# Two transformer blocks in fp32: the first projection unit of a layer before tile 1's transposes, and seven other operations moved

## The reference, cut to what matters

```python
for l in range(2):                                   # first block
    h = rmsnorm(x, pre_g[l]);  proj = h @ w_in[l]     # 2816 columns: u, v, g_a, q, k, v, g_b
    y_a = u * (spatial_w[l] applied to layernorm(v), + spatial_b) * silu(g_a)
    y_b = attention(rope(rmsnorm(q)), rope(rmsnorm(k)), v) * silu(g_b)     # 8 heads, 2 key heads
    x = x + rmsnorm(concat(y_a, y_b) @ w_out[l], post_g[l])
h = concat(zeros(112), meta_tokens(16), x)           # second block
proj = rms_norm(h, gain) @ w_in_2                    # 6400 columns
o_sb = stick_breaking_attention(8 heads)             # exp(log_beta + suffix sums of log(1 - beta))
o_sw = sliding_window_attention(16 heads, 2 key heads, sinks, rope)
merged = sigmoid(g_sb) * ((o_sb*silu(sb_z)) @ w_branch_sb) + sigmoid(g_sw) * ((o_sw*silu(sw_z)) @ w_branch_swa)
out = rms_norm(h + merged @ w_out_2, final_gain)     # rows of x alone
```

## Time and profile before

| what | value |
|---|---|
| profiled execution | 1017.53 us, span 1015.7 us, mean granted TensorE clock 0.997 |
| runs | 1016.79, 1018.24, 1018.8 us |
| TensorE (PE) busy | 982.3 us, 97% of the span |
| VectorE (DVE) busy | 618.0 us, 61% |
| ScalarE (ACT) busy | 497.8 us, 49% |
| GpSimd (POOL) busy | 265.0 us, 26% |
| DMA | 80.44 MB, 79 GB/s over the span |

### The profile page before, as it was taken

One profiled execution on the slowest core, in us unless ns is written; L12 is line 12 of the kernel. 1 busy time (PEld: TensorE's weight loads), 2 busy tenths in 40 slices (PEclk: granted clock), 3 DMA queues, 4 the chain that ended last, 5 costly groups with the idle time before them and its releaser, 6 DMA issues.

```text
span 1015.7 us, 13806 instructions
## 1 busy us (share of the span) xinstructions
PE 982.3 (97%) x5015; PEld 824.1 (81%) x5015; DVE 618.0 (61%) x917; ACT 497.8 (49%) x887; POOL 265.0 (26%) x198
## 2 busy tenths in 40 slices
PE   6999999999999999999999999999999989999996
PEld 5988888787888888787788889888787768888885
DVE  4777678928777678928336586588558962212204
ACT  4445656525445656525457577423557972222222
POOL 2216100003216100003322031140325764224242
PEclk9999999999999999999999999999999999999999
DMA  8332201231432101241322020023310003323312
GB/s 282 115 106 77 70 22 43 83 125 56 136 116 91 55 21 43 83 152 34 122 83 83 1 71 24 33 83 102 105 58 7 27 16 104 104 84 104 125 41 83
DMA packets 66790, 80.44 MB, mean 79 GB/s; under 512 B 5520, under 2 KB 50704, under 8 KB 66720
## 3 DMA queue, kind: packets, MB, share of 16 engines
q1 hardware_dynamic: 64816, 76.64, 23.4%
q10 hardware_dynamic: 1904, 2.88, 0.8%
HBM read 77.42 MB, written 2.10 MB: 78 GB/s over the span
## 4 chain that ended last, share of the span: by engine, by line
PE 56%; issue 29%; DVE 7%; ACT 4%; POOL 2%; DMA 1%; POOLq 0%; ACTq 0%; DVEq 0%
PE ps L1837 15%; PE ps L1839 15%; PE ps L1838 15%; DVE pwt L1516 2%; PE ps L1888 1%; PE ps L1890 1%; PE ps L1889 1%; PE ps L2175 1%; DVE wr L1613 1%; DVE yw L1732 1%; ACT whi L894 1%; PE ps L2323 1%; DMA x<-in_x 1%; POOL small L533 1%; POOL small L535 1%
## 5 line engine op out<-in xcount | busy, mean ns | idle before, releaser
L578 POOL TENSOR_TENSOR wlo<-raw,whi 128x2048 fp32r<-128x2048 f32 (+1 forms) x27 | 119.8, 4436 | 293.2 <-ACT whi L894 293.2
L1837 PE MATMUL ps<-whi,hhi 128*128 128x512 f32 (+1 forms) x320 | 116.4, 364 | 3.6 <-DVE wlo L1191 1.3
L1839 PE MATMUL ps<-whi,hlo 128*128 128x512 f32 (+1 forms) x320 | 114.9, 359 | 0.0
L1838 PE MATMUL ps<-wlo,hhi 128*128 128x512 f32 (+1 forms) x320 | 114.8, 359 | 0.0
L1837 PE MATMUL ps<-hhi,whi 128*128 128x512 f32 x288 | 113.3, 393 | 0.0
L1838 PE MATMUL ps<-hlo,whi 128*128 128x512 f32 x288 | 112.3, 390 | 0.0
L1839 PE MATMUL ps<-hhi,wlo 128*128 128x512 f32 x288 | 112.3, 390 | 0.0
L894 ACT ACTIVATE whi<-raw 128x2048 fp32r<-128x2048 f32 (+1 forms) x35 | 63.6, 1816 | 94.0 <-PE ps L1839 93.9
L660 ACT ACTIVATE whi<-raw 128x2048 fp32r<-128x2048 f32 (+1 forms) x29 | 52.2, 1800 | 72.8 <-PE ps L1839 72.8
L1191 DVE TENSOR_TENSOR wlo<-raw,whi 128x2048 fp32r<-128x2048 f32 (+1 forms) x29 | 63.6, 2192 | 35.9 <-ACT whi L660 35.1
L1888 PE MATMUL ps<-hhi,whi 128*128 128x512 f32 x192 | 78.2, 407 | 0.0
(11 more groups left out here) (310 smaller groups left out, 2332.4 us busy)
## 6 DMA issues: line engine op xcount, KB each, us to landing
raw<-in_w_in SPq DMA_DIRECT2D x42, 1024.0 KB, 5.3
raw<-in_w_out SPq DMA_DIRECT2D x12, 1024.0 KB, 5.0
raw<-in_w_in SPq DMA_DIRECT2D x10, 512.0 KB, 4.1
raw<-in_w_branch_swa SPq DMA_DIRECT2D x4, 1024.0 KB, 5.0
raw<-in_w_branch_sb SPq DMA_DIRECT2D x4, 512.0 KB, 3.4
x<-in_x ACTq DMA_DIRECT2D x3, 512.0 KB, 5.9
out<-x SPq DMA_DIRECT2D x3, 512.0 KB, 2.6
ws<-in_spatial_w SPq DMA_DIRECT2D x2, 512.0 KB, 6.7
```

Source lines behind the costliest of these rows:

```text
L578: pool.tensor_tensor(wlo[s][:, 0:n, :], raw[s][:, 0:n, :], whi[s][:, 0:n, :].bitcast(F32), ALU.subtract).then_inc(slab_split, 1)
L1837: pe.matmul(out_ap, lhsT=lhi(k), rhs=rhi(k), start=first and k == 0, stop=False, skip_group_check=True)
L1838: pe.matmul(out_ap, lhsT=lhi(k), rhs=rlo(k), start=False, stop=False, skip_group_check=True)
L1839: m = pe.matmul(out_ap, lhsT=llo(k), rhs=rhi(k), start=False, stop=last and k == n - 1, skip_group_check=True)
```

## The change

At the start of a layer unit (0,0) becomes a function, `first_unit`, that runs between the transposes of tile 0 and tile 1 at the program's start, and as the last thing in the loop's body for the layer (or block) that follows; the loops over `FIRST_UNITS` skip it. The identity transposes at the start become 12. ScalarE rounds the first piece of slab 0 ahead of tile 1's square sum, and VectorE takes its low part and tile 0's first half ahead of normalising tile 1. VectorE's low part of tile 3 moves from the loop's end to its top, and the low part of slab 2 ahead of the rope tables. `mix_low` and the gate's multiply move behind `read_head`. The meta tokens get a semaphore of their own. In the stick-breaking heads VectorE's `sb_read` moves ahead of `qk_parts`, and ScalarE's `copy_low_part` ahead of `meta_keys_hi` in head 1 and behind two copies at the end. The turned keys and queries are rounded ahead of a slab, and the low part of slab 34 moves from GpSimd to VectorE.

```diff
--- before
+++ after
@@ -358,6 +358,7 @@
         final_loaded = sem("final_loaded")
+        meta_loaded = sem("meta_loaded")
         start_done, consts_ready = sem("start_done"), sem("consts_ready")
@@ -494,7 +495,7 @@
             late(consts_f[:], a["consts"])
-            late(meta_row[:], a["meta_tokens_2"])
+            sp.dma_start(meta_row[:], a["meta_tokens_2"]).then_inc(meta_loaded, 16)
             for c in range(2):
@@ -622,9 +623,9 @@
             for j in range(21, len(SLABS2)):
-                if j in DVE_SLABS:
+                if j in DVE_SLABS or j == 34:
                     continue
-                if j - 1 in DVE_SLABS:
+                if j - 1 in DVE_SLABS or j == 35:
@@ -691,10 +692,10 @@
             sum_x(0, 0, 0)
+            first_slab_hi(0, 0, 0)
             act.wait_ge(x_loaded[1], 16)
...
             load_x(2)
-            first_slab_hi(0, 0, 0)
             load_x(3)
@@ -900,11 +901,12 @@
-            act.wait_ge(late_loaded, 128)
+            act.wait_ge(meta_loaded, 16)
             act.activation(junk[0:META, :], meta_row[:], ACT.Square, scale=ROOT, accum_out=small2[0:META, 0:1])\
...
             transposed_x(DEPTH, 0, 3)
+            act.wait_ge(late_loaded, 112)
             split2(2)
@@ -989,11 +991,11 @@
                         qk_parts(4 + h)
-                    if h == 1:
-                        meta_keys_hi(1)
                     if h in (4, 5):
...
                     copy_low_part(h)
+                    if h == 1:
+                        meta_keys_hi(1)
                 if h in (2, 3, 5):
@@ -1005,11 +1007,12 @@
             copy(sprm[:, 0, :], spm[:]).then_inc(sprm_hi, 1)
-            copy_low_part(7)
+            act.wait_ge(sbo_done, 8)
             for i in range(2):
...
                      ps[:, i, :].rearrange("p (t n) -> p t n", t=2)).then_inc(tokw_copied, 1)
+            copy_low_part(7)
             unit(29)
@@ -1046,10 +1049,10 @@
                 act.activation(tgz(c), ps[:, 6 + c % 2, :], ACT.Tanh, scale=0.5).then_inc(z_tanh, 1)
+                for p in TURNS_AT[c]:
+                    tokens_transposed_hi(p)
                 if c % 2 == 1 and c < 7:
                     split2(15 + c // 2)
-                for p in TURNS_AT[c]:
-                    tokens_transposed_hi(p)
             act.wait_ge(rope2_done, 5)
@@ -1195,9 +1198,9 @@
             normalise(0, 0, 0)
-            normalise(0, 0, 1)
             first_slab_low(0, 0, 0)
             transposed_x(0, 0, 0, (0,))
+            normalise(0, 0, 1)
             first_slab_low(0, 0, 1)
@@ -1205,8 +1208,9 @@
             transposed_x(0, 0, 2)
-            transposed_x(0, 0, 3)
             with dve.Fori(0, DEPTH) as l:
+                transposed_x(l, 0, 3)
+
                 count = [FIRST]
@@ -1218,6 +1222,7 @@
+                slab_low(l, 2)
                 dve.wait_ge(gain_loaded, l * 96 + 96)
@@ -1290,7 +1295,6 @@
-                slab_low(l, 2)
                 turned(0)
@@ -1395,6 +1399,13 @@
+                def open_gate(c):
+
+                    dve.wait_ge(gb_tanh, l * 4 + c + 1)
+                    dve.scalar_tensor_tensor(gb[:, c, :], eb[:, 1, :], 1.0, gb[:, c, :], ALU.add, ALU.mult)\
+                       .then_inc(gate_ready, 1)
+                    dve.wait_ge(gate_ready, l * 4 + c + 1)
+
                 def mix_slab_low_of(piece):
@@ -1430,12 +1441,17 @@
                     else:
+                        mix_low(2)
                         mix_slab_low_of(0)
...
                         read_head(h - 1)
+                    if h in (6, 7):
+                        mix_low(h - 6)
+                    if h % 2:
+                        open_gate(h // 2)
                     if h < 8:
@@ -1448,15 +1464,6 @@
                         probabilities_low(h, 3)
-                        if h >= 5:
-                            mix_low(h - 5)
-                        if h % 2 == 0:
-
-                            c = h // 2
-                            dve.wait_ge(gb_tanh, l * 4 + c + 1)
-                            dve.scalar_tensor_tensor(gb[:, c, :], eb[:, 1, :], 1.0, gb[:, c, :], ALU.add, ALU.mult)\
-                               .then_inc(gate_ready, 1)
-                            dve.wait_ge(gate_ready, l * 4 + c + 1)
@@ -1494,7 +1501,6 @@
                 transposed_x(l, 1, 2)
-                transposed_x(l, 1, 3)
                 a["chain"].append(count[0] - FIRST)
@@ -1516,9 +1522,10 @@
-            dve.wait_ge(late_loaded, 128)
             dve.wait_ge(meta_root, 1)
             dve.tensor_scalar(meta_row[:], meta_row[:], small2[0:META, 1:2], None, ALU.mult).then_inc(start_done, 1)
+            transposed_x(DEPTH, 0, 3)
+            dve.wait_ge(late_loaded, 112)
             dve.tensor_copy(rows_of[:], consts_f[:, CONSTS - 8:])
@@ -1615,6 +1622,7 @@
                     terms_lo(h + 1)
+                    sb_read(h)
                     if h < 4:
@@ -1627,8 +1635,8 @@
                     low(sprm[:, 1, :], spm[:], sprm[:, 0, :]).then_inc(sprm_lo, 1)
-                sb_read(h)
                 if h == 7:
+                    sb_read(h)
                     dve.wait_ge(meta_summed, 1)
@@ -1803,6 +1811,8 @@
+            slab2_low(34)
+
             def final_norm(t):
@@ -1851,9 +1861,23 @@
             pe.wait_ge(const_loaded, 16)
-            for n in range(16):
+            for n in range(12):
                 pe.matmul(ps[:, F_BANK, 0:P], lhsT=ident[:], rhs=ident[:], is_transpose=True)
+            def first_unit(l, ahead):
+
+                hi, lo = wide(whi[0]), wide(wlo[0])
+                pe.wait_ge(h_ready, l * 8 + ahead * 8 + 1)
+                for at_ in (0, 2):
+                    if at_ == 0:
+                        pe.wait_ge(first_low, l + ahead + 1)
+                    else:
+                        pe.wait_ge(slab_split, l * SLABS + ahead * SLABS + RING + 1)
+                    m = product(ps[:, 0, :], lambda k: hhi[:, at_ + k, 0:P], lambda k: hlo[:, at_ + k, 0:P],
+                                lambda k: hi[:, at_ + k, :], lambda k: lo[:, at_ + k, :], 2, first=at_ == 0, last=False)
+                m.then_inc(unit_done, 1)
+
             x_transposed(0, 0, 0)
+            first_unit(0, 0)
             x_transposed(0, 0, 1)
@@ -1871,8 +1895,6 @@
                     for at_ in (0, 2):
-                        if (i, t) == (0, 0):
-                            pe.wait_ge(*((slab_split, l * SLABS + RING + 1) if at_ else (first_low, l + 1)))
                         m = product(ps[:, t, :], lambda k: hhi[:, 4 * half + at_ + k, t * P:t * P + P],
@@ -1895,6 +1917,8 @@
                         x_transposed(l, 0, TILE_AT[n])
+                    if n == 0:
+                        continue
                     if (i, t) == (1, 0):
@@ -2048,6 +2072,7 @@
                         m.then_inc(unit_done, 1)
+                first_unit(l, 1)
@@ -2065,8 +2090,6 @@
                 for at_ in (0, 2):
-                    if (j, t) == (0, 0):
-                        pe.wait_ge(*((slab_split, DEPTH * SLABS + RING + 1) if at_ else (first_low, DEPTH + 1)))
                     m = product(ps[:, t, :], lambda k: hhi[:, 4 * half + at_ + k, tt],
```

## The result

The changed kernel takes 1025.38 us (median of 4 runs, 1024.32 to 1026.8) against 1017.64 before; the ratio is 1.0068, 95% interval 1.0053 to 1.0082. It is slower by about 7 us: 6.9 by the ratio, which is estimated from all runs and need not be the quotient of the medians, 7.7 by the medians. The profiled execution took 1024.32 us, 6.8 more than that of before.

The account below looks back on a forecast made before the run. TensorE, busy 982.3 of 1015.7 us, was taken as the bound, so only its idle stretches count; the terms sum to +5.2, giving 1022.7 on the profiled time and 1023.4 on the median, forecast 1023.0, range 1020.0 to 1026.2.

Parts of the forecast that it names:

- step 2: Third slab's low part ahead of rope tables: +1.1 us per layer at slab 4, -1.5 once at layer 1's slab 2.
- 1, opening: Program's start: first product no earlier, tile 1's displaced transposes, low part and slab 1 then paid, +3.0 us (1.5 to 4.2).
- step 3: Loop's turn: fewer queued matmuls cover TensorE's jump, +1.1 us; VectorE's tile 3 behind its jump 0, or 1.6 late.
- 4, 5, 7: Waits removed: first block's heads -2.0 us, second block's start (meta tokens) -1.35, keys rounded first -1.45, last copies -0.6.
- 6, heads: Stick-breaking heads: early read waits for ScalarE's copy and delays VectorE's queued work, +4.6 us, of it +3.4 in head 1.
- The clock: After head 1's gap of over 3 us the granted clock falls, slowing 6 matmuls: +1.2 us (0 to 1.7).
- rival A: Clock stays full in head 1's gap: 1021.8 us, chance 0.22 with the rival on slab 34 in it.
- 8, slab 34: Slab 34's low part moved to VectorE: 0 us (-1.4 to +1.0), the GpSimd wait being at slab 36.
- B: Slow jumps: TensorE's jump costs the 5.73 us of VectorE's idle time, VectorE late for tile 3; 1025.8, chance 0.12.
- C: The opening costs nothing, tile 1's transposes again filling a wait: 1020.0 us, chance 0.12.
- D: Head read not late, since ScalarE's copy ends in time: 1017.2 us, not slower, chance 0.09.
- E: Slab 34 was the wait on GpSimd: -1.4 us more, 1021.6, chance counted within the full-clock rival's 0.22.

Follow-up runs that it names:

- e6: Changed kernel with the opening's order restored on all three engines, the later layers' first unit still at the loop body's end: 1020.2 us, ratio 1.0017.
- e4: Changed kernel with the third slab's low part behind the rope tables again: 1021.56 us, ratio 1.0029.
- e8: Kernel before with one edit, VectorE's low part of tile 3 behind its jump to the loop's top: 1017.33 us, ratio 0.9988.
- e5: The changed kernel again, unchanged, as the measure for the other runs: 1024.44 us, ratio 1.0056.
- e7: e6 with each layer's first unit at the loop's top again, behind TensorE's jump: 1020.65 us, ratio 1.002.
- e10: e9 with slab 36's low part on VectorE instead of slab 34's: 1008.52 us, ratio 0.9911.
- e1: Changed kernel with the stick-breaking heads' read at its old place and the meta keys' rounding ahead of ScalarE's copy again: 1018.77 us, ratio 1.0008.
- e9: Changed kernel with heads' read, opening with first unit at the loop's top, and rope tables first all undone: 1011.8 us, ratio 0.9947.
- e2: Changed kernel with 12 TensorE multiplications by zeros filling head 1's gap: 1026.09 us, ratio 1.0061.
- e3: Changed kernel with head 1's read alone moved behind that head's key low parts: 1022.16 us, ratio 1.0033.

## Why the prediction was right

Direction and size held: +5.2 was forecast on the profiled time, +6.8 came; 1023.0 was said, 1025.38 measured, inside the range. Part of that is luck: three losses (opening, tables, clock) were put too low, but so were two gains (the first block's heads, the keys), and in step 2 one gain came from another edit than the one named. One reading at its start was wrong: there are waits over 1.5, on the identity (5.3), on pwt (1.8) and on xs (1.7); its sum uses none of them. By its steps:

- **1, opening:** forecast +3.0, measured about +3.4 (4.9 at slab 4 less that wait, 1.55). Mechanism as written: first product unmoved, transposes on the path, two waits of 1 behind them. e6 gave it back.
- **2, tables:** +1.1 a layer was +1.55 (a listed wait of 1.4 and 0.16). The 1.5 taken off for slab 2 of layer 1 did come off, but not through this edit: e4 kept it away without the edit, e8 got it without the rest. What did it was a line I had costed at nothing, VectorE's tile 3 put behind its jump (step 3). I had counted only what the moved part could lose. But the jump now begins 2.5 earlier (VectorE's idle time starts at 254.5 in e8, at 257.0 before), lies in time that VectorE would spend waiting for tile 3, and took less, 2.58 idle against 5.73. The right sum by cause: this edit +3.1, the jump's place -1.5. That the forecast's -1.5 came all the same is luck.
- **3, TensorE's jump:** forecast +1.1, measured 1.78 listed against 0.66 (1.33 in e5, 2.31 in e4). The two figures behind the forecast were both short: from the first of the 12 matmuls (244.49) to the product behind the jump (249.15) are 4.7, where 4.1 was chosen between 3.4 and 5.73, and the 12 take 2.7, not 2.4; the errors nearly cancel. The Trainium skill's rule on a taken branch out of the fetched pages ("Runtime: NRT & Kernel Launch", section Instruction fetch mechanics) fits: 0.46 idle with cover (e7), 1.78 with little. That the idle time is spent in fetching, no trace shows. The 108 ns of "Advanced Engine Details and Errata" in the Trainium skill (section Control Flow Timing) would explain neither.
- **4, 5, 7:** waits gone or shortened as named. The first block's heads gave 1.4 in each layer (the lag falls from 4.9 to 3.5 and from 4.65 to 3.3), not 1.0; meta tokens 1.3; keys 1.6 for 1.45; last copies 0.6.
- **6, heads:** +4.6 forecast, 0.4 + 3.45 + 0.4 measured; meta keys turned at 577.05, 5.9 later of which 2.0 was there already. The chain copy, read, low parts, mask is as written. **The clock** was the mis-sized term: +1.2 forecast from the 6 slow matmuls of the opening, 2.9 measured, since here the low level held for 6.8 us, 24 matmuls. I had put the upper bound at 1.7; it was too low, and rival A (clock stays full) was wrong.
- **8, slab 34:** 0, as forecast; the wait was slab 36's, and e10 removed it.

The measured terms add up: 3.4 + 1.6 + 1.1 - 2.8 - 1.3 + 4.25 + 2.9 - 1.6 - 0.6 = +6.95, against the profile's 6.8.

Rivals B, C, D and E did not occur. Step 6 with its clock is the loss: without it (e1) the change is worth nothing measurable either way, without the other two as well (e9) it is worth 0.5%. That the gains (heads, meta tokens, keys, last copies) come from their named edits is read from the waits; none was run by itself, so it is argued and not shown.

## What to carry to other kernels

An early wait costs what is queued behind it: before a read is moved up, find when its releaser ends, and list what stands between. Work that is ready (the tables) costs nothing ahead of a wait that comes anyway, and behind it 1.5 us each time here. And an idle stretch of the matmul engine of some 3 us cost up to as much again in clock afterwards; where it can't be removed, cheap matmuls in it can pay, if no other idle stretch takes its place.

## What was not expected

One jump of VectorE left it idle for 5.73 before and for 2.58 in e8. The longer one, from 257.0 to 262.75, began where the DMA engines were busiest: windows of the kernel before.

```profile
254.00:257.00 3.00, 3.00 (x18) 2.61 (x17) 2.20 (x4) 1.90 (x4) 0.00 (x0) 1.00 0.88 229
257.00:260.00 3.00, 3.00 (x15) 2.46 (x14) 0.02 (x1) 1.15 (x3) 0.00 (x0) 1.00 1.08 318
```

That the transfers lengthen a jump, whose code comes by DMA too (the page of the profile lists two instruction queues, 70 packets in all), fits but was not tested; e8's jump had a share of 0.92 beside it and was short.

Idle stretches of TensorE of nearly equal length had different ends: behind 2.2 us at the jump the clock fell in e2 and not in e4 (2.3), behind 1.9 in head 1 it stayed (e3), behind 3.3 it fell in each of the five profiles that had the gap unfilled, for 6.8 us in four and 3.4 in e7. And all kernels here, that of before too (822.61), have a wait of 1.8 on pwt between 813 and 831 us: in e2, e8 and e10 a low stretch follows it and costs 1.2 to 1.4, in the other eleven profiles none does. So a gap of 1.9 is not safe because it was in e3, and what decides is not settled by these runs. The opening's low stretch ended at 16 us in some profiles and at 20 in others, of the same order of work (e6 and e7).

These stretches are a good part of the 2 to 5 us by which single runs of one kernel differ. Of the 31 runs of the kernel before beside e1, the 13 with a mean granted clock of 0.993 to 0.995 took 1018.6 to 1021.9 us, the 18 with 0.997 and more 1015.7 to 1018.5. A single profile can thus mislead by 1 to 3 us in an edit's favour or against it; following the same matmul through both timelines shows where.
